# Expert routing of two mixture layers: group and experts in one pass, slots numbered from the last token, places weighted around the first unit

## The reference, cut to what matters

```
xn      = layer_norm(h)                         # gain and shift of the layer
logits  = xn @ [w_group | w_expert] + bias      # 4 group logits, 16 expert logits per token
g       = first argmax over the 4 group logits; pg = softmax(group logits)[g]
a, b    = first and second largest of the 4 expert logits of group g
wa, wb  = softmax([logit_a, logit_b]) * pg
h       = ALPHA * xn + sum over e in (a, b) of w_e * expert_e(xn)
expert  = (silu(x @ gate) * (x @ up)) @ down    # inner width 512
```

## Time and profile before

| | us |
|---|---|
| runs | 1682.50, 1680.33, 1682.51 (median 1682.5) |
| profiled execution, own time | 1680.41 |
| its span, first to last instruction | 1678.5 |
| PE busy | 1638.2 (98% of the span) |
| DVE busy | 895.9 (53%) |
| ACT busy | 697.9 (42%) |
| POOL busy | 5.0 (0%) |
| first mixture, from PE's first dummy product before the norm (L149) to the first gate product (L2401) | 1005.55 to 1026.18 |
| second mixture, the same | 1424.92 to 1445.27 |

### The profile page before, as it was taken

The page is one execution under the profiler, slowest core; times in us unless marked ns, Lnnn a source line. Parts: engine busy times, 40 slices in busy tenths (PEclk is TensorE's granted clock), DMA queues, the critical chain, the costliest instruction groups (busy, mean ns, idle before and its releaser), DMA issues.

```text
span 1678.5 us, 30194 instructions
## 1 busy us (share of the span) xinstructions
PE 1638.2 (98%) x12844; PEld 1281.2 (76%) x12844; DVE 895.9 (53%) x1932; ACT 697.9 (42%) x1350; POOL 5.0 (0%) x6
## 2 busy tenths in 40 slices
PE   9999999999999999999999999999989999999996
PEld 8889999787798699999887986555546798655553
DVE  6676565654467456568658765212136876521213
ACT  5576444433343354455557553111123655312111
POOL 0000000000000000000000000000000000000000
PEclk9999999999999999999999999999999999999999
DMA  8613453533201455434551546999992344699995
GB/s 344 251 76 151 158 219 126 183 107 144 90 4 51 191 187 194 184 131 177 195 201 32 189 172 259 426 423 426 426 413 81 106 188 172 262 426 424 426 424 232
DMA packets 36330, 372.15 MB, mean 222 GB/s; under 512 B 7264, under 2 KB 8416, under 8 KB 11360
## 3 DMA queue, kind: packets, MB, share of 16 engines
q1 hardware_dynamic: 32928, 364.09, 54.6%
q10 hardware_dynamic: 3264, 6.07, 1.2%
HBM read 369.09 MB, written 1.05 MB: 221 GB/s over the span
## 4 chain that ended last, share of the span: by engine, by line
PE 91%; DVE 6%; ACT 2%; issue 1%; DVEq 0%; ACTq 0%
PE ps L660 42%; PE ps L2401 13%; PE ps L2424 7%; PE ps L884 3%; PE ps L2413 2%; PE ps L1005 2%; PE ps L2384 2%; PE ps L1817 2%; PE ps L1786 2%; PE ps L986 1%; PE ps L437 1%; PE ps L2455 1%; PE ps L2888 1%; PE ps L1800 1%; PE ps L1570 1%; PE ps L997 1%
## 5 line engine op out<-in xcount | busy, mean ns | idle before, releaser
L660 PE MATMUL ps<-ffn_x_h,ffn_w 128*128 128x256 f32 x1408 | 257.4, 283 | 0.2
L2401 PE MATMUL ps<-ring,expert_inputs 128*64 128x256 f32 x1984 | 227.8, 382 | 0.0
L660 PEld LDWEIGHTS ps<-ffn_x_h,ffn_w 128*128 128x128 f32 x1408 | 221.3, 192 | 1.5 <-DVE ffn_x_l L499 0.5
L652 ACT CAST w_h<-ring 128x512 fp32r<-128x512 f32 x240 | 149.3, 624 | 138.2 <-PE ps L660 130.2
L655 DVE TENSOR_TENSOR w_l<-ring,w_h 128x512 fp32r<-128x512 f32 x240 | 164.0, 689 | 66.0 <-ACT w_h L652 62.1
L660 PE MATMUL ps<-ffn_x_l,ffn_w 128*128 128x256 f32 x704 | 199.2, 283 | 0.0
L2401 PEld LDWEIGHTS ps<-ring,expert_inputs 128*64 128x64 f32 x1984 | 137.0, 137 | 67.0
L655 DVE TENSOR_TENSOR ffn_w<-ring,ffn_w 128x1024 fp32r<-128x1024 f32 x132 | 155.7, 1220 | 20.9 <-ACT ffn_w L652 20.9
L660 PE MATMUL ps<-w_h,x_h 128*128 128x512 f32 x384 | 150.1, 391 | 0.0
L660 PE MATMUL ps<-w_h,x_l 128*128 128x512 f32 x384 | 149.5, 389 | 0.0
L660 PE MATMUL ps<-w_l,x_h 128*128 128x512 f32 x384 | 149.4, 389 | 0.0
(11 more groups left out here) (377 smaller groups left out, 2641.6 us busy)
## 6 DMA issues: line engine op xcount, KB each, us to landing
ring<-in_w_moe SPq DMA_DIRECT2D x62, 2048.0 KB, 14.0
ring<-in_w_proj SPq DMA_DIRECT2D x37, 2048.0 KB, 7.8
ring<-in_w_ffn SPq DMA_DIRECT2D x22, 3072.0 KB, 10.1
ring<-in_w_moe SPq DMA_DIRECT2D x64, 1024.0 KB, 14.5
ring<-in_w_b_in SPq DMA_DIRECT2D x1, 2496.0 KB, 12.9
ring<-in_w_lora SPq DMA_DIRECT2D x1, 2048.0 KB, 7.9
rows<-in_w_moe SPq DMA_DIRECT2D x2, 1024.0 KB, 9.8
h<-in_w_moe SPq DMA_DIRECT2D x2, 1024.0 KB, 4.8
```

Of the source, the lines that this page charges most:

```text
L652: act.copy(high, x).then_inc(ready.up(), 1)
L660: last = pe.matmul(out, a[x], b[y], start=start and n == 0, stop=stop and n == 2, skip_group_check=True)
L2401: last = pe.matmul(bank(0)[g * SLOTS_E:(g + 1) * SLOTS_E, 0:2 * P], x[:, k, e * SLOTS_E:(e + 1) * SLOTS_E], wg[g][:, k, :], start=(k == 0) ...
```

## The change

All of it is in `mixture`.

1. *Choice.* `first_max` runs once on all ten sets of four (for each block the group logits and the four groups of experts' logits) and once on the eight expert sets with the winners masked. The group's choice is applied afterwards, once, in `sel`.
2. *Slots.* Instead of numbering from the first token, slots are numbered from the last: `suffix = ones - tri` (made on DVE ahead of the logits, which now also wait for the constants there) counts the tokens from this one on. One product with `suffix` for both blocks and one with `ones` for the second block's counts into the first are left of five. The totals of an expert stand in the same result, as its maximum. `place` is made before the flag.
3. *Dummy products.* `fill(pe, 5, 2)` ahead of the counts goes, `fill(pe, 2, 2)` behind them becomes `fill(pe, 1, 2)`.
4. *`token_l`.* Of block 1 POOL makes features 0 to 511, behind its first subtraction, and DVE the rest. `low` now counts three.
5. *Weights.* The combination weights are made for each group's pair with the group's choice in `w1`, in fewer dependent steps.
6. *Order in `sparse`.* On DVE: features 2 and 3, weighting of EARLY, features 6 and 7, `put_places` LATE; the weighting of LATE comes in unit 0 behind the copy of the hidden rows.

```diff
@@ tensor
                     residual(0, range(KD))
-                    fill(pe, 5, 2)
                     pe.wait_ge(got.sem, got.at(48))
                     pe.wait_ge(chosen.sem, chosen.at(1))
-                    s0, s1 = [sel[:, t].rearrange("p g e -> p (g e)") for t in range(T)]
                     n = N_EXPERTS
-                    pe.matmul(bank(1)[:, 0:n], tri, s0, start=True, stop=True)
-                    for o, a in ((n, tri), (2 * n, ones)):
-                        pe.matmul(bank(1)[:, o:o + n], a, s1, start=True, stop=False)
-                        last = pe.matmul(bank(1)[:, o:o + n], ones, s0, start=False, stop=True)
-                    last.then_inc(mm.up(), 1)
-                    fill(pe, 2, 2)
+                    pe.matmul(bank(1)[:, 0:T * n], suffix, w[:, 224:256], start=True, stop=False, skip_group_check=True)
+                    pe.matmul(bank(1)[:, 0:n], ones, w[:, 224 + n:256], start=False, stop=True, skip_group_check=True).then_inc(mm.up(), 1)
+                    fill(pe, 1, 2)
...
-                        pe.wait_ge(low.sem, low.at(T))
+                        pe.wait_ge(low.sem, low.at(T + 1))
@@ vector
+                    dve.wait_ge(got.sem, got.at(48))
+                    dve.tensor_tensor(suffix, ones, tri, ALU.subtract)
                     dve.wait_ge(mm.sem, mm.at(2))
-                    dve.wait_ge(got.sem, got.at(48))
                     dve.tensor_tensor(lg, bank(4)..., bias..., ALU.add).then_inc(logits_read.up(), 1)
...
-                    first_max(lg[:, :, 0:4], gmx, gsel)
-                    dve.tensor_tensor(gexp, lg[:, :, 0:4], w4(gmx), ALU.subtract).then_inc(e_in.up(), 1)
-                    for t in range(T):
-                        el = lg[:, t, 4:ROUTE].rearrange("p (g e) -> p e g", g=4)
-                        ins = dve.tensor_tensor(eg[:, t], el, gsel[:, t:t + 1, :].broadcast_to([P, 4, 4]), ALU.mult)
-                    step(ins)
-                    step(dve.tensor_reduce(es, eg, AX, ALU.add))
-                    first_max(es, m1, oh1)
-                    step(dve.scalar_tensor_tensor(es2, oh1, MASKED, es, ALU.mult, ALU.add))
-                    first_max(es2, m2, oh2)
-                    dve.tensor_tensor(dm, m2, m1, ALU.subtract).then_inc(e_in.up(), 1)
-                    step(dve.tensor_tensor(tmp, oh1, oh2, ALU.add))
-                    for t in range(T):
-                        ... ins = dve.tensor_tensor(sel[:, t], tmp..., g, ALU.mult)
-                    ins.then_inc(chosen.up(), 1)
+                    first_max(logit_sets, m1, by_set(oh1))
+                    tops = by_row(m1)
+                    dve.tensor_tensor(gexp, lg[:, :, 0:4], tops[:, :, 0:1].broadcast_to([P, T, 4]), ALU.subtract).then_inc(e_in.up(), 1)
+                    step(dve.scalar_tensor_tensor(by_row(es2), first_of, MASKED, in_groups, ALU.mult, ALU.add))
+                    first_max(by_set(es2), m2, by_set(oh2))
+                    dve.tensor_tensor(dm, by_row(m2), tops[:, :, 1:N_GROUPS + 1], ALU.subtract).then_inc(e_in.up(), 1)
+                    step(dve.tensor_tensor(by_row(both), first_of, by_row(oh2), ALU.add))
+                    dve.tensor_tensor(sel, both..., over_four(gsel), ALU.mult).then_inc(chosen.up(), 1)
                     dve.wait_ge(high.sem, high.at(2))
-                    dve.tensor_tensor(parts_h[1][:, 1, :], h[:, 1, :], ...).then_inc(low.up(), 1)
+                    dve.tensor_tensor(parts_h[1][:, 1, 512:D], h[:, 1, 512:D], ...).then_inc(low.up(), 1)
                     dve.wait_ge(mm.sem, mm.at(3))
-                    step(dve.tensor_reduce(stat[:, 0:1], bank(1)[:, T * N_EXPERTS:(T + 1) * N_EXPERTS], AX, ALU.max))
+                    dve.tensor_reduce(stat[:, 0:1], bank(1)[:, 0:N_EXPERTS], AX, ALU.max)
+                    step(dve.tensor_tensor(place, bank(1)[:, 0:T * N_EXPERTS], w[:, 224:256], ALU.mult))
                     dve.tensor_scalar(overflow[:], stat[:, 0:1], float(SLOTS_E), None, ALU.is_gt).then_inc(known.up(), 1)
-                    step(dve.scalar_tensor_tensor(place, bank(1)[:, 0:T * N_EXPERTS], 1.0, w[:, 224:256], ALU.add, ALU.mult))
...
@@ vector, sparse
                             if m == 1:
-                                put_places(LATE, placed_late)
-                        dve.wait_ge(placed_late.sem, placed_late.at(1))
-                        for es_ in (EARLY, LATE):
-                            dve.tensor_tensor(put_w4..., put4..., by_expert(stat[:, 64:96], es_), ALU.mult).then_inc(put_weighted.up(), 1)
+                                weigh_places(EARLY)
+                        put_places(LATE, placed_late)
...
                             dve.tensor_copy(hids, ...).then_inc(hid_ready.up(), 1)
+                            if n == 0:
+                                dve.wait_ge(placed_late.sem, placed_late.at(1))
+                                weigh_places(LATE)
@@ gpsimd
+                    pool.wait_ge(high.sem, high.at(2))
+                    pool.tensor_tensor(parts_h[1][:, 1, 0:512], h[:, 1, 0:512], parts_h[0][:, 1, 0:512].bitcast(F32), ALU.subtract).then_inc(low.up(), 1)
@@ sync
-                    sp.wait_ge(low.sem, low.at(T))
+                    sp.wait_ge(low.sem, low.at(T + 1))
```

More of the change, by code:

```diff
@@ L2176, in mixture, with by_set, by_row @@
             wide = space.enter_context(nc.sbuf_tensor(f"expert_inputs{layer}", [P, 2 * BLK], F32))[:]
[L2177 to L2184, removed]
+            SETS = T * (N_GROUPS + 1)
+            def by_set(x):
+                return x.rearrange("p (a e) -> p a e", e=4)
+            def by_row(x):
+                return x.rearrange("p (t n) -> p t n", t=T)
+            logit_sets, oh1, key = by_set(w[:, 0:40]), w[:, 40:80], by_set(w[:, 80:120])
+            lg, gsel = by_row(w[:, 0:40]), by_row(oh1)[:, :, 0:4]
+            in_groups, first_of = lg[:, :, 4:ROUTE], by_row(oh1)[:, :, 4:ROUTE]
+            es2, oh2, both = w[:, 120:152], w[:, 152:184], w[:, 1680:1712]
+            gexp = by_row(w[:, 184:192])
+            m1, kmx, m2, dm, de, den = w[:, 416:426], w[:, 426:436], w[:, 436:444], by_row(w[:, 444:452]), by_row(w[:, 452:460]), by_row(w[:, 460:468])
+            w1, w2, gsum = by_row(w[:, 468:476]), by_row(w[:, 476:484]), w[:, 484:486]
+            suffix = w[:, 1024:1024 + P]
             comb = stat[:, 64:96].rearrange("p (t g e) -> p t g e", t=T, g=4)
@@ L2558, in w4, with by_four, over_four @@
                         return x.rearrange("p (t o) -> p t o", o=1).broadcast_to([P, T, 4])
-                    wr = rank.rearrange("p (o n) -> p o n", o=1).broadcast_to([P, T, 4])
+                    def by_four(x):
+                        return x.rearrange("p (a o) -> p a o", o=1).broadcast_to([P, x.shape[-1], 4])
+                    def over_four(x):
+                        return x.rearrange("p t (g o) -> p t g o", o=1).broadcast_to([P, T, 4, 4])
                     def first_max(x, m, onehot):
+                        a = x.shape[1]
+                        ranks = rank.rearrange("p (o n) -> p o n", o=1).broadcast_to([P, a, 4])
                         step(dve.tensor_reduce(m, x, AX, ALU.max))
[L2565 to L2568, removed]
+                        step(dve.tensor_tensor(key[:, 0:a], x, by_four(m), ALU.is_equal))
+                        step(dve.tensor_tensor(key[:, 0:a], key[:, 0:a], ranks, ALU.mult))
+                        step(dve.tensor_reduce(kmx[:, 0:a], key[:, 0:a], AX, ALU.max))
+                        step(dve.tensor_tensor(onehot, key[:, 0:a], by_four(kmx[:, 0:a]), ALU.is_equal))
                     norm_dve(dve, own_norm)
@@ L2588, in _ @@
-                    step(dve.tensor_reduce(es, eg, AX, ALU.add))
-                    first_max(es, m1, oh1)
-                    step(dve.scalar_tensor_tensor(es2, oh1, MASKED, es, ALU.mult, ALU.add))
-                    first_max(es2, m2, oh2)
-                    dve.tensor_tensor(dm, m2, m1, ALU.subtract).then_inc(e_in.up(), 1)
-                    step(dve.tensor_tensor(tmp, oh1, oh2, ALU.add))
-                    for t in range(T):
-                        g = gsel[:, t, :].rearrange("p (g o) -> p g o", o=1).broadcast_to([P, 4, 4])
-                        ins = dve.tensor_tensor(sel[:, t], tmp[:, t:t + 1, :].broadcast_to([P, 4, 4]), g, ALU.mult)
@@ L2598, in _ @@
+                    step(dve.tensor_tensor(by_row(both), first_of, by_row(oh2), ALU.add))
+                    dve.tensor_tensor(sel, both.rearrange("p (t g e) -> p t g e", t=T, g=4), over_four(gsel), ALU.mult).then_inc(chosen.up(), 1)
                     dve.wait_ge(high.sem, high.at(2))
-                    dve.tensor_tensor(parts_h[1][:, 1, :], h[:, 1, :], parts_h[0][:, 1, :].bitcast(F32), ALU.subtract).then_inc(low.up(), 1)
+                    dve.tensor_tensor(parts_h[1][:, 1, 512:D], h[:, 1, 512:D], parts_h[0][:, 1, 512:D].bitcast(F32), ALU.subtract).then_inc(low.up(), 1)
@@ L2615, in _ @@
                     step(dve.tensor_reduce(gsum, gexp, AX, ALU.add))
```

(16 more changed lines are left out.)

## The result

The changed kernel takes 1688.07 us (median of 10 runs, 1685.59 to 1690.30), the kernel before, on the same chips, 1682.45 us (10 runs, 1680.22 to 1685.92). The ratio is 1.003, 95% interval 1.0022 to 1.0039: **slower by 0.3%**, where 0.1% faster was forecast and 1684.4 was the end of the range.

What follows compares the result with a forecast made beforehand. PE, busy 98% of the span, was taken as the bound, waiting on DVE's choice, counts, places and flag in each expert layer. Layer sums of -1.04 and -0.72, together -1.7 us, gave 1680.8 us, range 1677.2 to 1684.4.

Steps and rivals of the forecast that it cites:

- The choice (term 0.0): DVE's expert choice: 1.59 us a layer saved alone, but spent waiting for POOL's subtractions, so no gain.
- Counting (-0.66): Counting products on PE: five of two passes become two, saving 0.66 us a layer.
- flag and branch (+0.08): Overflow flag sets the gather's start; `place` put ahead of it makes it 0.08 us later a layer.
- unit 0 (-0.46, -0.14): Late weighting moves behind unit 0's hidden rows, shortening PE's wait there: -0.46 us first layer, -0.14 second.
- the clock: Rival, 17%: without the ten dummies PE is nearly empty around the counts and its clock halves, 1.7 us a fall.
- it is broken in the middle by the counts: Argument against a clock fall: the counts interrupt PE's empty stretch ahead of the gather; no size given.
- both falls: PE's clock falling in both expert layers: +3.4 against the -1.7 forecast, +1.7 net, so 1684.2 us.
- what unit 0 gains, the rest gains: Behind unit 0's gate and up, PE runs gapless to the layer's end if weights come in time, keeping the gain.
- the first rival: PE's clock falls to half in both layers once the dummies are gone: 1684.2 us, 17%.
- port kept: Rival, 15%: POOL blocks DVE's two-SBUF-input operations over both subtractions, +0.65 us a layer, so 1682.1.

Runs made afterwards that it cites:

- e2: Changed kernel with nine dummy products put into the dense routine, which is not run, so PE's later code stands where it stood: 1682.82 us, ratio 1.0000.
- b1: Kernel before the change with 55 dummy products (220 PE instructions) put into the dense routine, which is not run: 1687.58 us, ratio 1.0031.
- e3: Changed kernel with POOL's second subtraction back on DVE, which makes all of block 1's `token_l`: 1686.03 us, ratio 1.0016.
- e4: Changed kernel with POOL's second subtraction back on DVE and `suffix` supplied as a constant: 1683.35 us, ratio 1.0007.
- e1: Changed kernel with the earlier dummy products back, five ahead of the counts and two behind them: 1687.51 us, ratio 1.0027.

## Why the prediction was wrong

- **The choice (term 0.0): right.** Measured +0.02 in each layer. The reading of two durations of L2565 as a block by POOL held to 0.05 us for operations not yet in the program.
- **Counting (-0.66), flag and branch (+0.08), unit 0 (-0.46, -0.14): right.** Measured -0.66 and -0.63 for the counts (0.02 of choice taken in); +0.01 and +0.08 from the counts to the gather, which starts 1.15 and 0.98 after the flag; unit 0 -0.48 and -0.15. POOL's second subtraction, for which only bounds of 1.2 to 1.5 were to be had, took 1.37. Together -1.83 for both layers, against -1.76 added up and -1.7 forecast.
- **First failed step, the clock: a rival at 17% that came true in both layers of the profile.** It was priced at 1.7 a fall and cost 1.47 and 1.34 there. What was set against it, "it is broken in the middle by the counts", did not hold: 0.6 us of small products and 0.55 of one dummy did not keep the clock up, here or in e2. "Cost nothing in time" of the dummies removed was right of the time that they take and wrong of what they hold. But this alone does not explain the result: with both falls the prediction's own sum is 1684.2, inside the range, and 3.9 us under what was measured.
- **Second failed step, and the larger: the place of the code, which the prediction put at nothing without a word.** "Behind that PE runs without a gap to the end of the layer; what unit 0 gains, the rest gains" stopped at the end of the layer. 36 instructions fewer moved a block border of PE's code into the transposes behind the mixture. Price: 4.6 us in the profile (4.77 less 0.2 of weights), 5.2 us in the medians of e2 against the changed kernel, 5.1 in b1 against the kernel before. For the profiled executions the account is -1.83 of steps, +2.81 of clock in the gathers, +4.77, and +0.45 of scatter: +6.2. From median to median it is +5.6; the scatter of the medians, about 1.5 us, is larger than what is left over.
- **Slips in the prediction's own figures.** The range's end, 1684.4, was called the first rival's value, which its sum gives as 1684.2. And the +3.0 of port kept and both falls lies below the 3.4 us that it was to pass. Neither touches the outcome.
- **Still open:** why the second block is fetched only some 6 us after the first, and whether the weight loads lengthen this. The DMA share in the changed kernel is 0.96 in 1256 to 1258, 0.55 in 1258 to 1260 and 0.27 in 1260 to 1261, so the block arrives as the loads end. No kernel with the loads held back was tried.

## What to carry to other kernels

When instructions are removed from an engine, look at where its code lies after the next taken branch: filling the routine that is not run with as many instructions adds no executed work and tells in one experiment whether a lost gain is a matter of place. Dummy products are judged by the nearly empty stretch that their removal leaves ahead of real work, not only by whether they hold anything up. And work moved to GpSimd must not run while DVE combines two SBUF tensors in a chain that sets the end.

## What the runs showed of the hardware that was not expected

- PE's wait for its own code is named "issue" in the waits and stands in the middle of a run of equal instructions: 2.4 to 2.8 us behind the 13th transpose in four kernels (changed, b1, e3, e4), 5.35 behind the first in one (e1). Two kernels with the same executed instructions differ by 5.1 us in the median (b1 and the kernel before).
- Behind the jump the two packets of code start 5.6 to 6.1 us apart in the five kernels of the table, also where PE had stood without instructions for 2.9 us (e1).
- A DVE operation with two SBUF inputs that is issued while POOL subtracts ends 0.03 to 0.16 us after the running POOL instruction, whenever it was issued (`suffix` took 0.84 and 0.99 us in the changed kernel, 1.13 in e3, 1.33 in e1, by its start). It gets through between two POOL instructions that are issued back to back: `suffix` ends at P+0.14 though POOL's second runs to P+1.30.
